# MLP blocks of a hybrid decoder step: which of VectorE and GpSimd makes the activations' sums, and which the weights'

## The chip, the cores and the metric

The kernel runs on one core of a Trainium2 chip. The metric is the device time of one execution in microseconds, and a version's time is the median over its runs. Engines are named as the profile names them: PE is TensorE (matmuls; PEld its weight loads), DVE is VectorE, ACT is ScalarE, POOL is GpSimd, SP is SyncE, which only issues DMAs here.

## What is computed

One layer of a decoder on 1024 prompt rows and 64 sample rows of width 1024, in float32: attention and a pooling branch, merged and projected, then an MLP. Only the MLP matters here. In the reference it is one line:

```
f = jnp.square(jax.nn.relu(rms_norm(h, g_pre_mlp) @ w_mlp_up)) @ w_mlp_down
return h + rms_norm(f, g_post_mlp)
```

The hidden width is 4096.

## The kernel before

Every float32 operand of a matmul is split into a high part (a copy rounded to the engine's fp32r type) and a low part (value minus high part), and each product is made of three matmuls: high by high, high by low, low by high. ACT makes high parts (tiles `wfh`, `wdh`), DVE low parts (`wfl`, `wdl`).

The MLP's hidden width is taken in blocks of 256 columns: 14 of them (`N_WINO`, the first written out, the other 13 in a loop on each engine), and a remainder of 4 tiles of 128 after them in the plain way. In a block, PE first makes the hidden activations (`wino_up`, six products of 8 input tiles), ACT applies relu and square (`wino_hidden`) into `wff`, and then PE multiplies them by two 128-row tiles of the down weights (`wino_downs`). This second product is made by Strassen's scheme in Winograd's form. For each of four groups `i` of row tiles it takes the four activation tiles A11, A12, A21, A22 and the four weight tiles B11 to B22, forms four sums of each (S1 to S4 from A, T1 to T4 from B), and needs seven products instead of eight. A product is named `(number, i)`: (5, 0) is product 5 of group 0. The sums are made in this kernel as follows.

- Of the activations: `wino_sums(w, i, squares)` on POOL, four additions of 128x128 elements for each group, 16 in a block. Group 3 needs the last squares of the block (`squares` 6), groups 1 and 2 those of the fourth product (4), group 0 those of the second (2).
- Of the weights: `wino_weight_sums(w)` on DVE, four additions of 128x512 elements in a block, once the weights have landed in `wdf`.

The results of the seven products leave PSUM in two ways. DVE adds five kinds of result into `acc` (`wino_add`). ACT copies the others into four small buffers `tmp` (`wino_copy`), from which POOL adds them into `acc` (`wino_pool_add`).

Each group has two PSUM banks, and products follow one another in them. So PE waits inside `wino_downs` before some products until a result was taken out: product (3, 0) waits for DVE's addition of (5, 0), product (6, 0) for ACT's copy of (1, 0). PE makes its products in pairs in this order: (1,0)(5,0), (1,1)(5,1), (6,0)(3,0), (6,1)(3,1), and so on; a pair is six matmuls of 512 columns.

Every engine executes its instructions in the order in which they are written, and waits on semaphores. `w_sq` counts ACT's squares, `w_sum` the activation sums, `wd_in` the weights' DMA, `wd_sum` the weight sums, `w_add` DVE's additions, `w_copy` ACT's copies. There is no scheduler: the order is that of the text.

Of the kernel before, what the change touches and what calls it, by code (L numbers as in the profile page):

```python
# [64 lines left out]
N_UP = len(W_UPS)  # L65
# [10 lines left out]
W_A21, W_A11, W_A22, W_A12, W_S1, W_S2, W_S3, W_S4 = range(8)  # L76
W_B12, W_B11, W_B21, W_B22, W_T1, W_T2, W_T3, W_T4 = range(8)
# [72 lines left out]
def build(nc, I, O):  # L150
    f32, f32r = mybir.dt.float32, mybir.dt.float32r
    ALU, ACT = mybir.AluOpType, mybir.ActivationFunctionType
    ctx = ExitStack()
    with ctx:
# [3 lines left out]
        def at(name, shape, off, dt=f32):  # L158
            return nc.alloc_sbuf_tensor_at(name, shape, dt, offset=16512 + off)
# [79 lines left out]
        wdf = at("wdf", [P, 8, 512], R32 + 16384)  # L239
        wfl = at("wfl", [P, 4, 8, P], R24, f32r)  # L240
        wff = at("wff", [P, 4, 8, P], R24)
# [27 lines left out]
        def sem(name):  # L269
            return ctx.enter_context(nc.semaphore(name))  # L270
# [28 lines left out]
        w_up, w_relu, w_sq, w_sum, w_fh, w_fl = (sem("w_" + n) for n in ("up", "relu", "sq", "sum", "f_hi", "f_lo"))  # L299
        wd_in, wd_sum, wd_hi, wd_lo = (sem("wd_" + n) for n in ("in", "sum", "hi", "lo"))  # L300
# [176 lines left out]
        def _(pool):  # L477
# [4 lines left out]
                               base=0, pattern=[[-1, P]], channel_multiplier=1).then_inc(ident_set, 1)  # L482
# [5 lines left out]
                               base=P - 1, pattern=[[-1, P]], channel_multiplier=-1).then_inc(consts, 1)  # L488
# [48 lines left out]
            def window(src, scratch, w, width, at_col):  # L537

                span, cur, n, i = 1, src, width + w - 1, 0
                base = at_col - (w - 1)  # L540
                while span < w:
                    n -= span
                    chained(pool.tensor_tensor(scratch[i % 2](0, n), cur(base + span, n), cur(base, n), ALU.add))
                    cur, base, span, i = scratch[i % 2], 0, 2 * span, i + 1
                return cur
# [8 lines left out]
            for t in range(PT_):  # L554
                w = 2 ** (t + 1)
                for c, (c0, width) in enumerate(CH):
                    width = min(width, SEQ - c0)
                    pool.wait_ge(freed["A"], FREED[g_in(U_UP + t, c)][1])
                    s = window(lambda a, n: upp[:, t, a:a + n], row, w, width, PSTATE + c0)
# [10 lines left out]
                s = window(lambda a, n: ups[:, t, :, a:a + n], per_seq, w, T_DEC, PSTATE)  # L570
# [29 lines left out]
            for i in range(3):  # L600
                pool.wait_ge(h_out[i], 16 * 3)

            def wino_sums(w, i, squares):

                a = lambda s: wff[:, i, s, :]
                base = w * 16 + 4 * i
                pool.wait_ge(w_sq, w * N_UP + squares)
                pool.tensor_tensor(a(W_S1), a(W_A21), a(W_A22), ALU.add).then_inc(w_sum, 1)  # L608
                pool.tensor_tensor(a(W_S3), a(W_A11), a(W_A21), ALU.subtract).then_inc(w_sum, 1)
                pool.wait_ge(w_sum, base + 1)  # L610
                pool.tensor_tensor(a(W_S2), a(W_S1), a(W_A11), ALU.subtract).then_inc(w_sum, 1)
                pool.wait_ge(w_sum, base + 3)
                pool.tensor_tensor(a(W_S4), a(W_A12), a(W_S2), ALU.subtract).then_inc(w_sum, 1)

            def wino_pool_add(w, m, first):

                number, i = m
                r = W_ROWS[i][0] if number == 4 else W_ROWS[i][1]
                k = W_COPIED[m]
                if number == 2:  # L620
                    pool.wait_ge(w_pool, w * N_COPY + (W_COPIED[(1, i)] + 1))
                pool.wait_ge(w_copy, copied_of(w, m))
                a = acc[:, r, 0:512]
                if first and number != 2:
                    pool.tensor_copy(a, tmp[k % N_TMP][:, :]).then_inc(w_pool, 1)
                else:
                    pool.tensor_tensor(a, a, tmp[k % N_TMP][:, :], ALU.add).then_inc(w_pool, 1)  # L627

            def wino_pool(w, first=False):
                wino_sums(w, 0, 2)  # L630
                wino_sums(w, 1, 4)
                wino_sums(w, 2, 4)
                wino_sums(w, 3, 6)
                wino_pool_add(w, (1, 0), first)
                wino_pool_add(w, (1, 1), first)
                wino_pool_add(w, (2, 0), first)
                wino_pool_add(w, (2, 1), first)
                wino_pool_add(w, (1, 2), first)
                wino_pool_add(w, (4, 0), first)
                wino_pool_add(w, (4, 1), first)  # L640
                wino_pool_add(w, (1, 3), first)
                wino_pool_add(w, (2, 2), first)
                wino_pool_add(w, (2, 3), first)
                wino_pool_add(w, (4, 2), first)
                wino_pool_add(w, (4, 3), first)
# [389 lines left out]
        def _(dve):  # L1035
# [299 lines left out]
            def wino_low(w, i):  # L1335
                dve.wait_ge(w_fh, w * 5 + (W_LO[i] + 1))
                if i == "sample":
                    dve.tensor_tensor(wsb[:, :, 1, :], wsf[:, :, :], wsb[:, :, 0, :].bitcast(f32), ALU.subtract)\
                        .then_inc(w_fl, 1)
                else:  # L1340
                    dve.tensor_tensor(wfl[:, i, 1:8, :], wff[:, i, 1:8, :], wfh[:, i, :, :].bitcast(f32), ALU.subtract)\  # L1341
                        .then_inc(w_fl, 1)

            def wino_weight_sums(w):
                b = lambda s: wdf[:, s, :]
                dve.wait_ge(wd_in, w * 32 + 32)
                dve.tensor_tensor(b(W_T1), b(W_B12), b(W_B11), ALU.subtract).then_inc(wd_sum, 1)
                dve.tensor_tensor(b(W_T3), b(W_B22), b(W_B12), ALU.subtract).then_inc(wd_sum, 1)
                dve.wait_ge(wd_sum, w * 4 + 1)
                dve.tensor_tensor(b(W_T2), b(W_B22), b(W_T1), ALU.subtract).then_inc(wd_sum, 1)  # L1350
                dve.wait_ge(wd_sum, w * 4 + 3)
                dve.tensor_tensor(b(W_T4), b(W_B21), b(W_T2), ALU.subtract).then_inc(wd_sum, 1)

            def wino_weights_low(w, half):
                s = slice(4 * half, 4 * half + 4)
# [5 lines left out]
            def wino_lo(w, s):  # L1361
                dve.wait_ge(w_hi, w * 2 + (U_W + 2 + s + 1))
                dve.tensor_tensor(wr[:, (s + 1) % 2, 1, :], raw[:, s, :], wr[:, (s + 1) % 2, 0, :].bitcast(f32),
                                  ALU.subtract).then_inc(w_lo, 1)

            def wino_add(w, m, first):

                number, i = m
                r = W_ROWS[i][1] if number in (6, 3) else W_ROWS[i][0]
                if number in (3, 7):  # L1370
                    dve.wait_ge(w_add, added_of(w, (6 if number == 3 else 5, i)))
                dve.wait_ge(w_done, done_of(w, m))
                a = acc[:, r, 512:]
                if first and number in (5, 6):
                    dve.tensor_copy(a, ps[:, wino_bank(m), :]).then_inc(w_add, 1)
                else:
                    dve.tensor_tensor(a, a, ps[:, wino_bank(m), :], ALU.add).then_inc(w_add, 1)  # L1377
# [7 lines left out]
                    dve.tensor_tensor(a, a, ps[:, 4:6, :], ALU.add).then_inc(w_add, 1)  # L1385

            def wino_from_lows(w, first=False):
                wino_low(w, 1)
                wino_low(w, 2)
                wino_low(w, "sample")  # L1390
                if first:
                    for i in range(3):
                        dve.wait_ge(h_out[i], 16 * 3)
                wino_add(w, (5, 0), first)
                wino_add(w, (5, 1), first)
                wino_add(w, (6, 0), first)
                wino_add(w, (3, 0), first)
                wino_add(w, (6, 1), first)
                wino_add(w, (3, 1), first)
                wino_add(w, (7, 0), first)  # L1400
                wino_add(w, (7, 1), first)
                wino_low(w, 3)
                wino_add(w, (5, 2), first)
                wino_lo(w, 0)
                wino_add(w, (5, 3), first)
                wino_add(w, (6, 2), first)
                wino_add(w, (3, 2), first)
                wino_add(w, (6, 3), first)
                wino_add(w, (3, 3), first)
                wino_add(w, (7, 2), first)  # L1410
                wino_add(w, (7, 3), first)
                wino_lo(w, 1)
                wino_sample_add(w, first)
# [4 lines left out]
            n_low(7)  # L1418
            normed(8)
            dve.wait_ge(done, G_M)  # L1420
            wino_weight_sums(0)
            n_low(8)
            wino_weights_low(0, 0)
            wino_low(0, 0)
# [1 line left out]
            dve.sem_inc(w_add, 1)  # L1426
            wino_from_lows(0, True)
            with dve.Fori(1, N_WINO) as w:
                wino_weight_sums(w)
                wino_weights_low(w, 0)  # L1430
                wino_low(w, 0)
                wino_weights_low(w, 1)
                wino_from_lows(w)
# [45 lines left out]
            for half, (ready, freeing) in enumerate(((y_half, y_part), (done, freed["D"]))):  # L1479
                cols = slice(half * 512, half * 512 + 512)  # L1480
                dve.wait_ge(ready, 1 if half == 0 else down_done(n))
                a, before_it = acc[:, r, cols], D0 + n
# [592 lines left out]
```

## Time and profile before

| | us |
|---|---|
| median of 3 runs | 1324.61 (1323.03 to 1325.12) |
| the profiled execution, its own time | 1320.92 |
| its span in the trace (first to last instruction) | 1319.2 |
| busy: PE | 1304.9 (99% of the span) |
| busy: DVE, ACT, POOL | 697.5, 569.2, 450.4 |

The span covers the instructions, and the execution's own time has 1.7 us around it. Busy time is the sum of an engine's instructions; that of PE is a model of overlapping matmuls, so 99% says that matmuls followed one another closely. PE's granted clock was 0.996 of full speed over the span.

### The profile page before, as it was taken

The page shows a single profiled execution, that of the slowest core. Times are in us where ns is not written, and L with a number is a line of the kernel's source. Part 1 is how long each engine was busy: PE and PEld are TensorE (multiplying, and loading weights), DVE is VectorE, ACT ScalarE, POOL GpSimd, SP SyncE. Part 2 cuts the span into 40 slices and gives each one's busy share as a digit, 9 for nine tenths or more (in the row PEclk, how much of TensorE's full clock was granted, in tenths as well). Part 3 has the DMA queues.
Part 4 walks back from the last instruction along what each step waited for, and adds up shares of the span by engine and source line. Part 5 has one row for each costly group of instructions (what it writes and reads, how often), then busy time and mean ns, then how long its engine had stood idle before and what let it go on. Part 6 is the DMA issues. An engine that isn't in the chain of part 4 may idle for free.

```text
span 1319.2 us, 20373 instructions
## 1 busy us (share of the span) xinstructions
PE 1304.9 (99%) x7483; PEld 1204.9 (91%) x7483; DVE 697.5 (53%) x1071; ACT 569.2 (43%) x1063; POOL 450.4 (34%) x541
## 2 busy tenths in 40 slices
PE   8999999999999999999999999999999999999998
PEld 7999889999999998889988998999899989998986
DVE  7488833222222245547567556656665666566256
ACT  7365524111111144436445544554455445544532
POOL 4002771000000001104466456645654575457010
PEclk9999989999999999999999999999999999999999
DMA  8200001111111125330110111011101110110152
GB/s 269 87 33 33 33 18 37 49 48 46 35 49 48 49 75 188 108 130 12 64 64 0 64 64 64 0 64 64 62 1 64 64 44 20 64 64 32 65 194 93
DMA packets 23638, 84.42 MB, mean 64 GB/s; under 512 B 3202, under 2 KB 3282, under 8 KB 23562
## 3 DMA queue, kind: packets, MB, share of 16 engines
q1 hardware_dynamic: 17968, 64.30, 13.9%
q0 software_dynamic: 5472, 19.12, 4.6%
q8 instruction: 37, 0.61, 0.2%
q10 hardware_dynamic: 146, 0.27, 0.1%
q14 instruction: 15, 0.12, 0.0%
HBM read 74.38 MB, written 10.39 MB: 64 GB/s over the span
## 4 chain that ended last, share of the span: by engine, by line
PE 94%; DVE 3%; ACT 2%; issue 1%; DMA 0%; DVEq 0%; ACTq 0%
PE ps L1878 20%; PE ps L1511 19%; PE ps L1512 19%; PE ps L1513 19%; PE ps L1753 9%; PE ps L1911 2%; PE ps L1532 2%; DVE pr L1153 1%; PE ps L1761 1%; ACT pr L771 1%; PE ps L1727 1%; PE ps L1670 0%; DVE pr L1191 0%; DMA xrow<-in_x_prompt 0%; PE ps L1828 0%
## 5 line engine op out<-in xcount | busy, mean ns | idle before, releaser
L1511 PE MATMUL ps<-xn,wr 128*128 128x384 f32 (+1 forms) x1360 | 448.1, 329 | 0.0
L1512 PE MATMUL ps<-xn,wr 128*128 128x384 f32 (+1 forms) x1360 | 445.9, 328 | 0.0
L1513 PE MATMUL ps<-xn,wr 128*128 128x384 f32 (+1 forms) x1360 | 445.6, 328 | 0.0
L1511 PEld LDWEIGHTS ps<-xn,wr 128*128 128x128 f32 x1360 | 256.8, 189 | 1.0
L1512 PEld LDWEIGHTS ps<-xn,wr 128*128 128x128 f32 x1360 | 256.8, 189 | 0.6
L1513 PEld LDWEIGHTS ps<-xn,wr 128*128 128x128 f32 x1360 | 256.6, 189 | 0.0
L627 POOL TENSOR_TENSOR acc<-acc,tmp 128x512 f32<-128x512 f32 x160 | 239.5, 1518 | 46.6 <-ACT tmp L947 44.7
L1377 DVE TENSOR_TENSOR acc<-acc,ps 128x512 f32<-128x512 f32 x216 | 143.4, 685 | 37.8 <-PE ps L1878 31.2
L947 ACT ACTIVATE tmp<-ps 128x512 f32<-128x512 f32 x168 | 97.2, 597 | 150.8 <-PE ps L1878 120.3
L1878 PE MATMUL ps<-wdh,wfh 128*128 128x512 f32 x392 | 130.4, 390 | 0.0
L1878 PE MATMUL ps<-wdl,wfh 128*128 128x512 f32 x392 | 130.1, 390 | 0.0
L1878 PE MATMUL ps<-wdh,wfl 128*128 128x512 f32 x392 | 129.8, 389 | 0.0
L1039 DVE TENSOR_TENSOR wr<-raw,wr 128x1024 fp32r<-128x1024 f32 x36 | 44.5, 1236 | 143.3 <-ACT wr L666 143.3
L608 POOL TENSOR_TENSOR wff<-wff 128x128 f32<-128x128 f32 x56 | 35.2, 628 | 214.7 <-ACT wff L919 175.0
L911 ACT ACTIVATE fa<-ps 128x384 f32<-128x384 f32 (+1 forms) x84 | 39.8, 474 | 147.0 <-PE ps L1513 147.0
L582 POOL DMA_DIRECT2D g<-in_vectors x3 | 1.7, 566 | 280.6 <-DVE mix L1224 267.2
L1341 DVE TENSOR_TENSOR wfl<-wff,wfh 128x896 fp32r<-128x896 f32 x56 | 65.0, 1173 | 59.8 <-ACT wfh L928 59.8
L1359 DVE TENSOR_TENSOR wdl<-wdf,wdh 128x2048 fp32r<-128x2048 f32 x28 | 64.2, 2292 | 56.1 <-ACT wdh L936 56.1
L1878 PEld LDWEIGHTS ps<-wdh,wfl 128*128 128x128 f32 x392 | 73.6, 188 | 15.7
L1878 PEld LDWEIGHTS ps<-wdl,wfh 128*128 128x128 f32 x392 | 73.6, 188 | 15.4
L1878 PEld LDWEIGHTS ps<-wdh,wfh 128*128 128x128 f32 x392 | 73.0, 188 | 14.8 <-ACT tmp L947 0.4
L1753 PE MATMUL ps<-wo,xn 128*128 128x512 f32 x336 | 77.7, 390 | 0.0
(280 smaller groups left out, 1835.9 us busy)
## 6 DMA issues: line engine op xcount, KB each, us to landing
raw<-in_weights SPq DMA_DIRECT2D x78, 512.0 KB, 4.1
wdf<-in_weights SPq DMA_DIRECT2D x28, 512.0 KB, 4.1
xrow<-in_x_prompt SPq DMA_DIRECT2D x8, 512.0 KB, 8.6
xr<-in_x_prompt POOLq DMA_DIRECT2D x8, 512.0 KB, 5.4
residual_rows<-h POOLq DMA_DIRECT2D x8, 512.0 KB, 2.9
hb<-residual_rows POOLq DMA_DIRECT2D x8, 512.0 KB, 9.8
out_y_prompt<-hb SPq DMA_DIRECT2D x7, 512.0 KB, 2.6
g<-in_vectors POOLq DMA_DIRECT2D x3, 512.0 KB, 4.0
```

The source lines that it names most:

```text
L627: pool.tensor_tensor(a, a, tmp[k % N_TMP][:, :], ALU.add).then_inc(w_pool, 1)
L911: act.activation(f[:, 0:width], ps[:, W_BANK[i], 0:width], ACT.Relu).then_inc(w_relu, 1)
L947: act.activation(tmp[k % N_TMP][:, :], ps[:, wino_bank(m), :], ACT.Copy).then_inc(w_copy, 1)
L1039: dve.tensor_tensor(lo_, raw[:, n % 2, :], hi_.bitcast(f32), ALU.subtract).then_inc(w_lo, 1)
L1341: dve.tensor_tensor(wfl[:, i, 1:8, :], wff[:, i, 1:8, :], wfh[:, i, :, :].bitcast(f32), ALU.subtract)\
L1359: dve.tensor_tensor(wdl[:, s, :], wdf[:, s, :], wdh[:, s, :].bitcast(f32), ALU.subtract).then_inc(wd_lo, 1)
L1377: dve.tensor_tensor(a, a, ps[:, wino_bank(m), :], ALU.add).then_inc(w_add, 1)
L1511: pe.matmul(out, wh, rh, start=(i == 0), stop=False)
L1512: pe.matmul(out, wh, rl, start=False, stop=False)
L1513: mm = pe.matmul(out, wl, rh, start=False, stop=(i == last))
L1753: mm = [pe.matmul(out[:, half, :], s, m[:, half * 512:(half + 1) * 512], start=start, stop=stop) for half in range(2)]
L1878: return pe.matmul(ps[:, wino_bank(m), :], s, v, start=number in (1, 5, 2) and part == 0, stop=part == 2, skip_group_check=True)
```

## The change

The two helpers change places. POOL's text gets `wino_weight_sums` at the head of each block, and loses the four calls of `wino_sums`. DVE's text loses `wino_weight_sums`, and gets `wino_sums` in four places: group 0 where the weight sums were, groups 1 and 2 ahead of their low parts, and group 3 behind the low part of the samples, ahead of the block's first addition. The sums themselves are the same. ACT's and PE's texts are unchanged.

```
 POOL:
+            def wino_weight_sums(w):
+                b = lambda s: wdf[:, s, :]
+                pool.wait_ge(wd_in, w * 32 + 32)
+                pool.tensor_tensor(b(W_T1), b(W_B12), b(W_B11), ALU.subtract).then_inc(wd_sum, 1)
+                pool.tensor_tensor(b(W_T3), b(W_B22), b(W_B12), ALU.subtract).then_inc(wd_sum, 1)
+                pool.wait_ge(wd_sum, w * 4 + 1)
+                pool.tensor_tensor(b(W_T2), b(W_B22), b(W_T1), ALU.subtract).then_inc(wd_sum, 1)
+                pool.wait_ge(wd_sum, w * 4 + 3)
+                pool.tensor_tensor(b(W_T4), b(W_B21), b(W_T2), ALU.subtract).then_inc(wd_sum, 1)
...
             def wino_pool(w, first=False):
-                wino_sums(w, 0, 2)
-                wino_sums(w, 1, 4)
-                wino_sums(w, 2, 4)
-                wino_sums(w, 3, 6)
+                wino_weight_sums(w)
                 wino_pool_add(w, (1, 0), first)
                 wino_pool_add(w, (1, 1), first)
...
 DVE:
+            def wino_sums(w, i, squares):
+
+                a = lambda s: wff[:, i, s, :]
+                base = w * 16 + 4 * i
+                dve.wait_ge(w_sq, w * N_UP + squares)
+                dve.tensor_tensor(a(W_S1), a(W_A21), a(W_A22), ALU.add).then_inc(w_sum, 1)
+                dve.tensor_tensor(a(W_S3), a(W_A11), a(W_A21), ALU.subtract).then_inc(w_sum, 1)
+                dve.wait_ge(w_sum, base + 1)
+                dve.tensor_tensor(a(W_S2), a(W_S1), a(W_A11), ALU.subtract).then_inc(w_sum, 1)
+                dve.wait_ge(w_sum, base + 3)
+                dve.tensor_tensor(a(W_S4), a(W_A12), a(W_S2), ALU.subtract).then_inc(w_sum, 1)
...
             def wino_from_lows(w, first=False):
+                wino_sums(w, 1, 4)
+                wino_sums(w, 2, 4)
                 wino_low(w, 1)
                 wino_low(w, 2)
                 wino_low(w, "sample")
+                wino_sums(w, 3, 6)
...
             with dve.Fori(1, N_WINO) as w:
-                wino_weight_sums(w)
+                wino_sums(w, 0, 2)
                 wino_weights_low(w, 0)
```

How DVE's instructions stand in the loop, from the samples' low part (`wsb`) to the additions of (5, 0) and (5, 1) into `acc`. Before:

```order
L1338 TENSOR_TENSOR wsb<-wsf,wsb 128x2x64 [waits w_f_hi]
L1372 ISA
L1377 TENSOR_TENSOR acc<-acc,ps 128x512 [waits w_product]
L1372 REGISTER_ALU
L1377 TENSOR_TENSOR acc<-acc,ps 128x512 [waits w_product]
```

With the change, at the same place:

```order
L1333 TENSOR_TENSOR wsb<-wsf,wsb 128x2x64 [waits w_f_hi]
L1343 REGISTER_ALU
L1344 TENSOR_TENSOR wff<-wff 128x128 [waits w_sq]
L1345 TENSOR_TENSOR wff<-wff 128x128
L1346 REGISTER_ALU
L1347 TENSOR_TENSOR wff<-wff 128x128 [waits w_sum]
L1348 REGISTER_ALU
L1349 TENSOR_TENSOR wff<-wff 128x128 [waits w_sum]
L1369 ISA
L1374 TENSOR_TENSOR acc<-acc,ps 128x512 [waits w_product]
```

Group 3's four sums (S1, S3, S2, S4 in this order) now stand between the samples' low part and the addition of (5, 0).

How POOL's instructions stand in the loop, at the end of group 3's sums and the first two additions from `tmp`, which are those of (1, 0) and (1, 1). Before:

```order
L607 REGISTER_ALU
L608 TENSOR_TENSOR wff<-wff 128x128 [waits w_sq]
L609 TENSOR_TENSOR wff<-wff 128x128
L610 REGISTER_ALU
L611 TENSOR_TENSOR wff<-wff 128x128 [waits w_sum]
L612 REGISTER_ALU
L613 TENSOR_TENSOR wff<-wff 128x128 [waits w_sum]
L622 ISA
L627 TENSOR_TENSOR acc<-acc,tmp_125 128x512 [waits w_copied]
L622 REGISTER_ALU
L627 TENSOR_TENSOR acc<-acc,tmp_126 128x512 [waits w_copied]
```

With the change, the whole head of POOL's loop:

```order
L606 TENSOR_TENSOR wdf<-wdf 128x512 [waits wd_in]
L607 TENSOR_TENSOR wdf<-wdf 128x512
L608 ISA
L609 TENSOR_TENSOR wdf<-wdf 128x512 [waits wd_sum]
L610 REGISTER_ALU
L611 TENSOR_TENSOR wdf<-wdf 128x512 [waits wd_sum]
L620 ISA
L625 TENSOR_TENSOR acc<-acc,tmp_125 128x512 [waits w_copied]
L620 REGISTER_ALU
L625 TENSOR_TENSOR acc<-acc,tmp_126 128x512 [waits w_copied]
```

Nothing stands between the weight sums and the additions from `tmp` any more, so the addition of (1, 0) waits for ACT's copy alone.

## Rows read from the trace of the kernel before

**Rows 1.** The page, busy time and the chain that ended last

```profile
PE 1304.9 (99%) x7483; PEld 1204.9 (91%) x7483; DVE 697.5 (53%) x1071; ACT 569.2 (43%) x1063; POOL 450.4 (34%) x541
...
PE 94%; DVE 3%; ACT 2%; issue 1%; DMA 0%; DVEq 0%; ACTq 0%
```

**Rows 2.** What PE waited for, longest first: us in total, times, longest

```profile
PE ps L1532 <- DVE pr L1191: 2.5, 4, 1.3
```

**Rows 3.** Single lines: durations in ns (min/median/max), first and last start in us

```profile
L608 POOL TENSOR_TENSOR wff<-wff x56: 460/462/1859, 601.2 to 1196.7; 128x128 f32<-128x128 f32 x56
...
L627 POOL TENSOR_TENSOR acc<-acc,tmp x160: 1286/1298/2289, 623.6 to 1218.3; 128x512 f32<-128x512 f32 x160
...
L1377 DVE TENSOR_TENSOR acc<-acc,ps x216: 674/687/690, 620.6 to 1212.9; 128x512 f32<-128x512 f32 x108
...
L1138 DVE TENSOR_TENSOR vd<-vr x7: 283/284/291, 59.6 to 60.9; 128x128 f32<-128x128 f32 x7
...
L1338 DVE TENSOR_TENSOR wsb<-wsf,wsb x14: 309/313/314, 617.7 to 1197.0; 128x128 fp32r<-128x128 f32 x14
```

**Rows 4.** Timeline of DVE in one block: start us, us, what [idle before]

```profile
840.34 0.31 DVE L1338 TENSOR_TENSOR wsb<-wsf,wsb 128x128 fp32r<-128x128 f32 x1 [0.89 <-ACT wsb L925]
840.57 0.68 DVE L1377 TENSOR_TENSOR acc<-acc,ps 128x512 f32<-128x512 f32 x1
```

**Rows 5.** Timeline of PE in the same block, the pair (6, 0) and (3, 0)

```profile
841.26 0.39 PE L1878 MATMUL ps<-wdh,wfl 128*128 128x512 f32 x1
841.49 0.61 PE L1878 MATMUL ps<-wdh,wfh 128*128 128x512 f32 x2
```

**Rows 6.** Timeline in the first block: PEld's waits, and DVE's copy of (5, 0)

```profile
617.90 0.68 DVE L1375 COPY acc<-ps 128x512 f32<-128x512 f32 x1
...
618.63 0.19 PEld L1878 LDWEIGHTS ps<-wdh,wfh 128*128 128x128 f32 x1 [0.27 <-DVE acc L1375]
618.74 0.19 PEld L1878 LDWEIGHTS ps<-wdl,wfh 128*128 128x128 f32 x1
```

**Rows 7.** Timeline of ACT: copies of (1, 0), (1, 1) and (2, 0)

```profile
840.21 0.58 ACT L947 ACTIVATE tmp<-ps 128x512 f32<-128x512 f32 x1
841.46 0.60 ACT L947 ACTIVATE tmp<-ps 128x512 f32<-128x512 f32 x1 [0.68 <-PE ps L1878]
...
845.77 0.60 ACT L947 ACTIVATE tmp<-ps 128x512 f32<-128x512 f32 x1 [1.89 <-PE ps L1878]
```

**Rows 8.** Timeline of POOL: the addition of (2, 0)

```profile
846.45 1.30 POOL L627 TENSOR_TENSOR acc<-acc,tmp 128x512 f32<-128x512 f32 x1 [1.99 <-ACT tmp L947]
```

**Rows 9.** Timeline in the first block: DVE and POOL additions side by side

```profile
600.79 0.68 DVE L1347 TENSOR_TENSOR wdf<-wdf 128x512 f32<-128x512 f32 x1
601.39 0.95 DVE L1348 TENSOR_TENSOR wdf<-wdf 128x512 f32<-128x512 f32 x1
...
601.15 0.64 POOL L608 TENSOR_TENSOR wff<-wff 128x128 f32<-128x128 f32 x1 [2.52 <-DMA residual_rows<-h]
601.76 0.90 POOL L609 TENSOR_TENSOR wff<-wff 128x128 f32<-128x128 f32 x1
```

**Rows 10.** Timeline of the block of rows 4, its earlier part: DVE and POOL

```profile
820.55 0.69 DVE L1347 TENSOR_TENSOR wdf<-wdf 128x512 f32<-128x512 f32 x1 [5.45 <-DMA wdf<-in_weights]
...
824.78 0.46 POOL L608 TENSOR_TENSOR wff<-wff 128x128 f32<-128x128 f32 x1 [6.47 <-ACT wff L919]
...
826.63 2.29 DVE L1359 TENSOR_TENSOR wdl<-wdf,wdh 128x2048 fp32r<-128x2048 f32 x1 [3.46 <-ACT wdh L936]
829.74 1.09 DVE L1341 TENSOR_TENSOR wfl<-wff,wfh 128x896 fp32r<-128x896 f32 x1 [0.82 <-ACT wfh L928]
...
837.31 2.13 DVE L1341 TENSOR_TENSOR wfl<-wff,wfh 128x896 fp32r<-128x896 f32 x2 [3.47 <-ACT wfh L928]
```

**Rows 11.** Stretches: us, busy of PE, PEld, DVE, ACT, POOL; then PE's granted clock

```profile
180.00:185.60 5.60, 5.60 (x68) 4.86 (x66) 0.30 (x1) 0.58 (x1) 5.12 (x7) 1.00 0.30 97
185.60:192.50 6.90, 6.90 (x37) 6.67 (x38) 0.42 (x1) 0.38 (x1) 4.88 (x6) 0.51 0.00 0
```

More of the change, by code:

```diff
@@ L601, in _ @@
                 pool.wait_ge(h_out[i], 16 * 3)
[L603 to L613, printed above, removed]
+            def wino_weight_sums(w):
[7 more added lines that the diff above has]
+                pool.tensor_tensor(b(W_T4), b(W_B21), b(W_T2), ALU.subtract).then_inc(wd_sum, 1)
             def wino_pool_add(w, m, first):
@@ L1342, in wino_low @@
                         .then_inc(w_fl, 1)
[L1344 to L1352, printed above, removed]
+            def wino_sums(w, i, squares):
[8 more added lines that the diff above has]
+                dve.tensor_tensor(a(W_S4), a(W_A12), a(W_S2), ALU.subtract).then_inc(w_sum, 1)
             def wino_weights_low(w, half):
@@ L1420, in _ @@
             dve.wait_ge(done, G_M)
-            wino_weight_sums(0)
+            wino_sums(0, 0, 2)
             n_low(8)
```

## The prediction

> **What bounds the kernel now.** I read the page's busy times first. PE is busy for 99% of the span and makes 94% of the chain that ended last [rows 1]. Next comes the list of PE's waits: its largest entry is 2.5 us, and it lies in the attention part, not in the MLP [rows 2]. So PE's own work sets the time. Work taken off DVE, ACT or POOL gains nothing, and the only question is whether the change makes PE wait. The 13 blocks of the loop repeat very evenly: the samples' low part, once per block, takes 309 to 314 ns each time and runs from 617.7 to 1197.0, which is 44.6 us per block [rows 3]. So one block, read closely, speaks for 13.
>
> Where could PE wait? The place to look at is its third pair, (6, 0)(3, 0). The first matmul of (6, 0) starts at 841.49; two in a row take 0.61 and one alone 0.39, so that of (3, 0) starts at 841.49 + 0.61 - 0.39 = 841.71 [rows 5]. The weights of (3, 0) are loaded beside the matmul in front, from 841.49 on, and this load carries the wait for DVE's addition of (5, 0). That addition runs from 840.57 to 841.25 [rows 4]. The first block shows what happens when it is late: the copy ends at 618.58, the weights start loading 0.05 later, marked as a wait on it, and the matmul starts with the next load, 0.11 later [rows 6]. So today's slack is 841.49 - 841.25 - 0.05 = 0.19 us, and behind it each microsecond on DVE is one on PE.
>
> **The change, part by part.**
>
> *Weight sums, DVE to POOL.* They start when the DMA has landed, at 820.55 [rows 10]. POOL has been idle since 824.78 - 6.47 = 818.31 [rows 10]. A 128x512 addition takes POOL 1.30 us against DVE's 0.69 [rows 3, 10]; four take about 4 x 1.25 + 0.2 = 5.2 us (successive ones overlap by some 0.05, and two wait for a result; an estimate), so they end near 825.8. The first reader is DVE's first low part of the weights at 826.63, and behind that DVE has another 0.82 us idle [rows 10]. Cost 0. What hides it is 0.8 + 0.8 us of other engines' work; were it gone, each microsecond would be one per block.
> The Trainium skill, GPSIMD Engine Reference, section Engine selection, advises against this half of the change: elementwise work on VectorE, since GpSimd is about twice as slow with two inputs. The rows agree on the ratio (1.30 to 0.69), and off the path it costs nothing.
>
> *Activation sums, POOL to DVE.* A 128x128 addition takes DVE 0.28 us [rows 3]. The next one starts 0.08 us before the end of the one in front, as the addition at 840.57 does before 840.65 [rows 4], so a step is 0.20, and 0.31 where it waits for the result in front. Four take about 0.9 us. Group 0 goes where the weight sums were: its squares are ready at 824.7, since POOL takes them up at 824.78 [rows 10]. POOL's fourth weight sum may hold it up until 825.8, then it ends near 826.7, against 826.63; hidden by the 0.82 idle. Groups 1 and 2 fall into the 3.47 us that DVE idles ahead of 837.31 [rows 10] and need 1.8. Cost 0. Group 3 has no such gap: it stands between the samples' low part and the addition of (5, 0).
>
> *Group 3 with nothing in the way.* S1 takes the place of the addition, 840.57; S3 840.77; S2 840.97; S4 waits for S2's end at 841.25 and runs 841.28 to 841.56; the addition starts at 841.48 and ends at 842.16. PE's matmul follows 0.05 + 0.11 later, at 842.32 instead of 841.71: 0.6 us per block.
>
> *Group 3 beside POOL.* But POOL is no longer busy with these sums. Its first addition from `tmp`, today behind them, waits only for ACT's copy, which ends at 840.79 [rows 7]. POOL starts 0.08 after a copy, as 846.45 follows 845.77 + 0.60 [rows 7, 8], so at 840.87, in the middle of the sums.
> What two such operations do to one another is seen in the first block, where both engines have two inputs in SBUF [rows 9]. DVE's addition from 600.79 ends at 601.47. POOL's from 601.15 takes 0.64 instead of 0.46 [rows 3] and ends at 601.79, 0.32 after DVE's. DVE's next starts at 601.39, takes 0.95 instead of 0.69 and ends at 602.34, 0.55 after POOL's. POOL's next ends at 602.66, again 0.32 after that. So each holds the other out to its end, in turn, even where DVE had its next instruction queued already; and an operation needs whatever is shared only 0.14 us after its start (0.46 - 0.32, and 0.69 - 0.55). DVE's additions out of PSUM are not touched: 216 of them take 674 to 690 ns [rows 3].
> The Trainium skill, SBUF — State Buffer, section SBUF: two separate sides, says the same of a DVE operation with two SBUF inputs and a GpSimd one: an exclusive lock for the whole instruction, to the one that starts first. By it the sum is the one that follows, about 1360; without it, 1332.
> Carried through: S1 ends at 840.85, S3 holds until 841.06. POOL's (1, 0) asks at 841.01, S2 at 841.11, so POOL goes first and holds 1.30 - 0.14 = 1.16, to 842.22. S2 ends at 842.36. ACT's copy of (1, 1) ends at 842.06 [rows 7]; POOL starts (1, 1) at 842.17, just before the end of (1, 0), and asks at 842.31. S4 asks only at 842.53, for it waits for S2. So POOL takes the second turn, to 843.52, S4 ends at 843.66, the addition of (5, 0) runs 843.58 to 844.26, and PE's matmul comes at 844.42 instead of 841.71. Cost 2.7 us per block. The bounds are 0.6 (no contention) and 2.7 (two turns; POOL has no third addition ready before PE goes on). I take the upper one, since the rows of the first block are the same kind of pair.
>
> *Behind it.* Waits after this point hang on PE's own later products and move with it. DVE has (5, 1) done by 844.9, and PE's pair (6, 1)(3, 1) then stands near 845.5. The next block starts with every engine in the same relation to PE. Nothing takes up the 2.7 us, for PE is idle nowhere in the block.
>
> *First block.* PE waits there already [rows 6], and its first additions are copies. Between 0 and 2.7; I take 0.5.
>
> *Sum.* 13 x 2.7 + 0.5 = 35.6 us. On the profiled execution (1320.9) that is 1356.5; on the median, 3.7 us above it, 1324.6 + 35.6 = 1360.
>
> **The rivals.**
>
> *One turn only (B).* If POOL's (1, 1) asks after S4, that is 0.22 us later than worked out, the addition ends one hold earlier. S4 then ends at 842.67, the addition at 843.27, the matmul comes at 843.43: 1.7 us per block, 13 x 1.7 + 0.5 = 22.6, 1347. For it: the margin is small. Against: the copies' times repeat within nanoseconds from block to block, as the low part's durations suggest.
>
> *No contention (C).* If the short sums slip through, 13 x 0.6 = 7.8, 1332. For it: 0.28 us operations are much shorter than any that the rows show held up on DVE. Against: POOL's 0.46 us ones were held up.
>
> *Not slower (D).* The addition of (5, 0) has 0.19 us of slack. If DVE finished the four sums that much earlier, or they cost under 0.19 in all, PE would not wait, and the first block's wait, which hangs partly on POOL's late sums, would go: 1324.1. It decides at 0.05 us per sum, against a step of 0.20. Hardly possible.
>
> *The clock falls (E).* PE would idle 2.7 us at once in each block, more than the four waits of the largest entry of its list together [rows 2]. At 185.6 to 192.5 the granted clock was 0.51, the lower level of 1.2 GHz [rows 11]; such a fall costs half of 6.9, 3.4 us. Against: ahead of this fall, from 180 to 185.6, PE was not waiting but busy with 68 small matmuls at a clock of 1.00, 2.4 GHz [rows 11], so the trace ties no fall to a single wait, nor does it rule one out. If it fell in a third of the blocks: 4.3 x 3.4 = 15 more, 1375; in all of them 45 more, 1405.
>
> **How the numbers follow.** Chances: two turns 0.50, B 0.14, C 0.12, D 0.05, E 0.19. The likeliest gives 1360. The range 1343 to 1385 holds the first two and most of E (0.14 of 0.19), 0.78 in all; C and D lie below it, the worst of E above. The likeliest case alone has 1355 to 1366: 0.2 us of error per block is 2.6. A measurement of this kernel tells about 0.2%, 2.6 us, from no change. Only D is not beyond it: faster 0.01, same 0.04, slower 0.95.
>
> **What would show it.** In the list of PE's waits: a new entry, DVE's `acc` addition, 13 or 14 times, 2.5 to 2.7 us each, and block lengths of 47.3 instead of 44.6. On DVE: S2 and S4 of group 3 at about 1.4 us each instead of 0.28, S1 and S3 plain. On POOL: (1, 0) starting 0.53 us after the samples' low part. Weight sums on POOL at 1.3 us each, with nobody waiting for them. C would show four plain sums and PE waits of 0.6, B one long S2 or S4 and 1.7, E a granted clock under 1.00 in the MLP. I would be wrong if PE waited for `wdl` or `wfl` instead, or if DVE kept the shared side through its chain of sums.

## The result, and the profile after

The changed kernel takes 1365.69 us (median of 4 runs, 1362.74 to 1367.65) against 1324.38 for the kernel before: a ratio of 1.0319, interval 1.0305 to 1.0333, 41.3 us more. Forecast were 1360 and slower. Ratios are estimated together with their intervals, and can differ in the last digit from the quotient of two medians. Four executions ran in a slow state (1449.86 and 1890.97 us in two of the experiments, 2625.2 and 3365.72 of the kernel before beside them) and are left out of all times and ratios.

The page, busy time and the chain that ended last, as in [rows 1]:

```profile
PE 1315.1 (96%) x7483; PEld 1208.6 (89%) x7483; DVE 747.7 (55%) x1239; ACT 568.9 (42%) x1063; POOL 412.7 (30%) x373
...
PE 89%; DVE 5%; ACT 3%; issue 2%; DMA 1%; DVEq 0%; SPq 0%; ACTq 0%
```

PE has the same 7483 matmuls, but its share fell from 99% to 96%, and DVE now has 5% of the chain. The list of PE's waits, as in [rows 2], names the place:

```profile
PE ps L1878 <- DVE acc L1374: 30.7, 13, 2.4
...
PE ps L1878 <- DVE acc L1372: 0.6, 1, 0.6
```

There are 13 waits for DVE's addition into `acc`, one for each block of the loop, and a short one in the first block. The list counts from the modelled end of the matmul in front, so its 2.4 us is less than a block loses by the wait (2.7 us, below). Here is the place in one block, on DVE, as in [rows 4]:

```profile
856.56 0.29 DVE L1333 TENSOR_TENSOR wsb<-wsf,wsb 128x128 fp32r<-128x128 f32 x1 [0.93 <-ACT wsb L920]
856.77 0.28 DVE L1344 TENSOR_TENSOR wff<-wff 128x128 f32<-128x128 f32 x1
856.97 0.28 DVE L1345 TENSOR_TENSOR wff<-wff 128x128 f32<-128x128 f32 x1
857.17 1.37 DVE L1347 TENSOR_TENSOR wff<-wff 128x128 f32<-128x128 f32 x1
858.58 1.23 DVE L1349 TENSOR_TENSOR wff<-wff 128x128 f32<-128x128 f32 x1
859.74 1.27 DVE L1374 TENSOR_TENSOR acc<-acc,ps 128x512 f32<-128x512 f32 x2
```

And on POOL, as in [rows 8]:

```profile
857.09 1.30 POOL L625 TENSOR_TENSOR acc<-acc,tmp 128x512 f32<-128x512 f32 x1 [15.10 <-ACT tmp L942]
...
858.36 1.30 POOL L625 TENSOR_TENSOR acc<-acc,tmp 128x512 f32<-128x512 f32 x1
```

Read them side by side. S1 and S3 take their plain 0.28 us. POOL's addition of (1, 0) starts at 857.09, while S3 is in work, and ends at 858.39; S2, started at 857.17, ends at 858.54. POOL's addition of (1, 1) ends at 859.66, S4 at 859.81. Each of the two sums ends 0.15 us after an addition of POOL. The addition of (5, 0) starts 3.18 us after the samples' low part, instead of 0.23 [rows 4]. PE feels it like this, as in [rows 5], one block earlier:

```profile
810.43 0.39 PE L1878 MATMUL ps<-wdh,wfh 128*128 128x512 f32 x1
813.18 0.50 PE L1878 MATMUL ps<-wdh,wfh 128*128 128x512 f32 x1 [2.36 <-DVE acc L1374]
```

The matmul of (3, 0) starts 2.75 us after that of (6, 0), where it was 0.22, and takes 0.50 us itself instead of 0.39. The samples' low parts of these two blocks stand 856.56 - 809.27 = 47.29 us apart, against 44.6 before:

```profile
809.27 0.29 DVE L1333 TENSOR_TENSOR wsb<-wsf,wsb 128x128 fp32r<-128x128 f32 x1 [0.93 <-ACT wsb L920]
...
905.33 0.29 DVE L1333 TENSOR_TENSOR wsb<-wsf,wsb 128x128 fp32r<-128x128 f32 x1 [0.93 <-ACT wsb L920]
```

The last row is the block after them: it stands 905.33 - 856.56 = 48.77 us behind, 1.5 us more than 47.29.

That block is one of four with another mark: PE's granted clock. The columns are those of [rows 11].

```profile
716.92:720.34 3.42, 3.18 (x8) 2.51 (x9) 1.73 (x4) 1.52 (x2) 0.00 (x0) 0.50 0.00 0
860.28:863.70 3.42, 3.23 (x8) 2.56 (x9) 1.73 (x4) 1.47 (x2) 0.00 (x0) 0.50 0.00 0
1003.64:1007.06 3.42, 3.33 (x8) 2.66 (x9) 1.73 (x4) 1.36 (x2) 0.00 (x0) 0.50 0.00 0
1147.00:1150.42 3.42, 3.36 (x8) 2.69 (x9) 1.73 (x4) 1.34 (x2) 0.00 (x0) 0.50 0.00 0
```

In every third block PE ran at the lower level (0.50, 1.2 GHz) for 3.42 us. Each stretch begins 0.06 to 0.24 us before PE's wait ends (3.42 less PE's busy time in it), and PE starts 8 matmuls in it. At full clock matmuls start 0.227 us apart, so 14 or 15 would fit. The four blocks with a fall are 48.73 to 48.83 us long and the others, behind the first, 47.25 to 47.29 (from the starts of the samples' low parts), so a fall costs 1.5 us, 6.0 in all.

The first block costs little. PE's second product starts there at 615.25 and in the next block at 660.38, 45.13 us later. With the change it starts at 618.80 and 664.38, 45.58 us apart: 0.45 more.

So the 41.3 us are 13 x 2.7 = 35 of waiting, 6.0 of clock and about 0.5 in the first block; the sum is 41.5. What lies ahead of the MLP differs by a few us between executions, whatever the kernel: that second product starts at 615.81 in the first experiment below and at 618.88 in the last, whose texts agree up to there, and the runs of the kernel before go from 1317.94 to 1326.04. It is left aside.

### The profile page after: what moved, and what is told of

Read it like the earlier page. It is cut to its first block, busy times and chain, and to the rows that moved or that the text cites. A ratio compares the mean times of both kernels' runs of the same rounds, so it can differ in the third digit from the quotient of the medians.

```text
span 1364.1 us, 20373 instructions
## 1 busy us (share of the span) xinstructions
PE 1315.1 (96%) x7483; PEld 1208.6 (89%) x7483; DVE 747.7 (55%) x1239; ACT 568.9 (42%) x1063; POOL 412.7 (30%) x373
## 4 chain that ended last, share of the span: by engine, by line
PE 89%; DVE 5%; ACT 3%; issue 2%; DMA 1%; DVEq 0%; SPq 0%; ACTq 0%
PE ps L1511 18%; PE ps L1512 18%; PE ps L1513 18%; PE ps L1878 17%; PE ps L1753 9%; PE ps L1532 2%; PE ps L1911 2%; DVE wff L1347 1%; DVE pr L1148 1%; PE ps L1761 1%; DMA xrow<-in_x_prompt 1%; DVE acc L1374 1%; ACT pr L766 1%; PE ps L1727 1%; ACT fa L906 0%
## 5 line engine op out<-in xcount | busy, mean ns | idle before, releaser
L1878 PE MATMUL ps<-wdh,wfh 128*128 128x512 f32 x392 | 136.9, 402 | 31.4 <-DVE acc L1374 30.7
L1374 DVE TENSOR_TENSOR acc<-acc,ps 128x512 f32<-128x512 f32 x216 | 142.5, 684 | 41.3 <-PE ps L1878 34.7
L1344 DVE TENSOR_TENSOR wff<-wff 128x128 f32<-128x128 f32 x56 | 25.7, 458 | 125.3 <-ACT wff L914 125.3
L1753 PEld LDWEIGHTS ps<-wo,xn 128*128 128x128 f32 x336 | 63.0, 188 | 13.4
```

The costliest lines, as they stand in the source:

```text
L1753: mm = [pe.matmul(out[:, half, :], s, m[:, half * 512:(half + 1) * 512], start=start, stop=stop) for half in range(2)]
L1878: return pe.matmul(ps[:, wino_bank(m), :], s, v, start=number in (1, 5, 2) and part == 0, stop=part == 2, skip_group_check=True)
```

## The experiments

**Group 3's sums alone given back to GpSimd.** In the changed kernel:

```
 POOL, wino_pool:
                 wino_weight_sums(w)
+                wino_sums(w, 3, 6)
                 wino_pool_add(w, (1, 0), first)
 DVE, wino_from_lows:
                 wino_low(w, "sample")
-                wino_sums(w, 3, 6)
```

> The changed kernel with the sums of group 3 alone given back to GpSimd, where they stand behind the weight sums and ahead of the first addition from tmp; the sums of groups 0 to 2 stay on VectorE and the weight sums on GpSimd. Theory (the loss comes from group 3's sums alone, which VectorE makes in turns with GpSimd's additions): nothing is left of it, 1324 us, no entry in PE's list of waits for VectorE's additions in the loop, granted clock 1.00 in the MLP. Rival (weight sums on GpSimd, or the other sums on VectorE, carry a part): between 1330 and 1365, with PE waiting for wdl or wfl. Rival (any move of work off GpSimd's queue lets its additions collide with VectorE): some of the 2.7 us per block stays.

1322.05 us, ratio to the kernel before 0.9998 (0.998 to 1.0015). Nothing of the loss is left, and the clock stays at full speed. The other 12 sums on DVE and the weight sums on POOL, together, cost nothing.

**Group 3's sums alone on VectorE.** In the kernel before:

```
 POOL, wino_pool:
                 wino_sums(w, 2, 4)
-                wino_sums(w, 3, 6)
 DVE, wino_from_lows:
                 wino_low(w, "sample")
+                wino_sums(w, 3, 6)
```

> The kernel before, with group 3's sums alone moved to VectorE, to the place that the change gives them; everything else, the weight sums on VectorE too, as before. Theory: the whole loss, as in the changed kernel: 13 x 2.7 = 35, and some 1.5 us for each block in which the granted clock falls, so 1360 to 1367. Rival (the loss needs the weight sums on GpSimd as well, or the other groups on VectorE): clearly less, 1332 if only the 0.6 us of the longer queue counts.

1367.27 us, ratio 1.032 (1.0295 to 1.0344), the whole loss. The waits of PE in the loop are the same to the last digit:

```profile
PE ps L1890 <- DVE acc L1388: 30.7, 13, 2.4
```

The clock fell here too, for 3.42 us in each of four blocks, every third (from 719.17, 862.53, 1005.89 and 1149.25). The first block waits 1.6 us instead of 0.6.

**The weight sums alone on GpSimd.** In the kernel before:

```
 POOL, wino_pool:
+                wino_weight_sums(w)
                 wino_sums(w, 0, 2)
 DVE, loop and first block:
-                wino_weight_sums(w)
```

> The kernel before, with the weight sums alone moved to GpSimd, ahead of its activation sums; VectorE loses them and gets nothing. Theory: four additions of 1.3 us that end before anyone needs them, and GpSimd's additions from tmp still behind its own sums: 1324, same as before. Rival (GpSimd's slower additions are felt): group 0's sums start about 1 us later and ScalarE's high part with them; if that reached PE, up to 1 us per block, 1337.

1334.06 us, ratio 1.0083 (1.006 to 1.0107). The theory gave 1324 and was wrong. POOL's list had room for the weight sums, but the activation sums behind them now start later and meet DVE's low parts, which have two inputs in SBUF as well. In the first block POOL comes to its second activation sum just when DVE starts a long low part; the first two rows are DVE's and POOL's, and the third, from PE's weight loads, shows what came of it:

```profile
607.70 2.47 DVE L1360 TENSOR_TENSOR wdl<-wdf,wdh 128x2048 fp32r<-128x2048 f32 x1 [0.58 <-POOL wdf L611]
...
607.98 2.51 POOL L619 TENSOR_TENSOR wff<-wff 128x128 f32<-128x128 f32 x1
...
620.48 0.50 PEld L1877 LDWEIGHTS ps<-wdh,wfh 128*128 128x128 f32 x2 [4.04 <-issue]
```

A sum of 0.46 us took 2.51, and it ended 0.32 after DVE's low part. PE's weight loads stood still for 4 us at the start of the second product. The profile names no releaser for that wait ("issue"); that the first block's weight sums bring it is shown by the next run, which has them on VectorE and no such wait. PE's clock was 0.50 for 6.8 us, from 0.8 us before the wait ended:

```profile
619.70:626.50 6.80, 5.99 (x14) 4.77 (x15) 3.29 (x5) 3.66 (x8) 3.64 (x7) 0.50 0.00 0
```

In the loop, too, sums meet low parts. Group 0's last sum falls behind one of the weights and takes 2.39 us (first row, POOL). Everything behind it on POOL comes later, and the last sum of group 2 meets the low part of group 1 (rows of DVE, POOL and ACT):

```profile
836.56 2.39 POOL L623 TENSOR_TENSOR wff<-wff 128x128 f32<-128x128 f32 x1
...
847.00 1.09 DVE L1352 TENSOR_TENSOR wfl<-wff,wfh 128x896 fp32r<-128x896 f32 x1 [2.93 <-ACT wfh L939]
...
847.11 1.30 POOL L623 TENSOR_TENSOR wff<-wff 128x128 f32<-128x128 f32 x1
...
848.44 0.95 ACT L939 ACTIVATE wfh<-wff 128x896 fp32r<-128x896 f32 x1 [1.48 <-POOL wff L623]
```

ACT idles 1.48 us for it, and what ACT does next is late too: PE's weight loads now wait in each block of the loop for ACT's copy (up to 0.4 us) and for DVE's addition (up to 0.3). The blocks are about 0.4 us longer (45.0).

**The same, in the loop only,** with the first block's weight sums left on VectorE:

```
 POOL, wino_pool:
+                if not first:
+                    wino_weight_sums(w)
                 wino_sums(w, 0, 2)
```

> The run with the weight sums alone on GpSimd took 10 us more than before. Here they are on GpSimd in the 13 blocks of the loop, and on VectorE in the first block as before. Theory (two losses: in the first block GpSimd starts late and its sums meet VectorE's low parts, one long wait of PE and a fall of the granted clock, 4 to 6 us; in each block of the loop group 2's last sum meets VectorE's low part of group 1, 0.37 us): 13 x 0.37 = 5, 1329, no fall of the clock near the first block. Rival (all of it comes from the first block and its echo in the later ones): 1324. Rival (all from the loop): 1334.

1327.46 us, ratio 1.0047 (1.0024 to 1.007). The samples' low part again gives the blocks: (1203.8 - 617.4) / 13 = 45.1.

```profile
L1350 DVE TENSOR_TENSOR wsb<-wsf,wsb x14: 307/311/313, 617.4 to 1203.8; 128x128 fp32r<-128x128 f32 x14
```

By the two ratios, the 11 us of the run before fall into 6 of the loop (uncertain by 3) and 5 of the first block (by 4). No long wait and no fall of the clock is left in the first block, and the ratio is above 1 by more than its interval, so both losses exist. The loss in the loop was expected a little lower (0.37 a block, now 0.5).

**GpSimd's additions held until group 3's sums are done.** In the changed kernel, one wait more:

```
 POOL, wino_pool:
                 wino_weight_sums(w)
+                pool.wait_ge(w_sum, w * 16 + 16)
                 wino_pool_add(w, (1, 0), first)
```

> The changed kernel with one wait more on GpSimd: its first addition from tmp waits until group 3's four sums are done (w_sum), so that none of its additions can run beside them. Nothing is taken away; GpSimd starts later. Theory (turns at something shared): the sums take 0.28 us each again and only the longer queue counts, 0.6 us per block, 13 x 0.6 = 8, 1332, granted clock 1.00. Rival (the sums are slow on VectorE by themselves, or the place in the queue is the cost): 1365 as in the changed kernel, since VectorE's and PE's texts are the same.

1333.31 us, ratio 1.0071 (1.0053 to 1.0089). One wait more takes 32 us off. VectorE:

```profile
802.52 0.29 DVE L1345 TENSOR_TENSOR wff<-wff 128x128 f32<-128x128 f32 x1
802.73 0.28 DVE L1346 TENSOR_TENSOR wff<-wff 128x128 f32<-128x128 f32 x1
802.93 0.28 DVE L1348 TENSOR_TENSOR wff<-wff 128x128 f32<-128x128 f32 x1
803.25 0.29 DVE L1350 TENSOR_TENSOR wff<-wff 128x128 f32<-128x128 f32 x1
803.46 1.28 DVE L1375 TENSOR_TENSOR acc<-acc,ps 128x512 f32<-128x512 f32 x2
```

All four sums are plain: from the first one's start to that of the addition it is 0.94 us, against 0.9 worked out from a step of 0.20. What is left, 0.6 us per block, is the price of the place in the queue.

**Only the second addition held.** The same wait ahead of `wino_pool_add(w, (1, 1), first)` instead:

> The changed kernel with GpSimd's second addition from tmp, (1, 1), held until group 3's sums are done; its first, (1, 0), runs as it likes. Theory (the two engines take turns, and each of GpSimd's additions that falls among the sums costs one hold of 1.16 us, less what the plain chain takes): one turn instead of two, S2 long and S4 plain, 1.6 to 1.7 us of waiting per block, 13 x 1.65 = 21, 1346, plus at most a few us if the granted clock still falls. Rival (one turn costs all, the second is hidden): 1360 to 1365. Rival (only the second counts): 1332.

1347.11 us, ratio 1.0169 (1.0144 to 1.0194). One sum is long, the other plain:

```profile
853.27 1.37 DVE L1348 TENSOR_TENSOR wff<-wff 128x128 f32<-128x128 f32 x1
854.67 0.29 DVE L1350 TENSOR_TENSOR wff<-wff 128x128 f32<-128x128 f32 x1
```

So each addition of POOL among the sums is one turn. Two turns, one and none give 41, 22 and 9 us. In the profiled execution of this run the granted clock never fell in the MLP, so its 22 us are waiting alone; of the 41 us, 6.0 are clock.

**Matmuls that fill PE's wait.** In the changed kernel, in the pair (6, 0)(3, 0); the ten products are written to a bank that is overwritten later and are used for nothing, and the wait on `w_relu`, which counts ACT's relus, keeps them off what ACT has still to read:

```
                 wino_term(m, 0)
...
+                if fill:
+                    pe.wait_ge(w_relu, w * N_UP + 3)
+                    for _ in range(fill):
+                        pe.matmul(ps[:, 0, :], wfh[:, 0, 0, :], wdh[:, 1, :], start=True, stop=True, skip_group_check=True)
                 bank_read(w, n)
```

> The changed kernel with ten matmuls of 512 columns more in each block on PE, between the first product of (6, 0) and the wait for VectorE's addition of (5, 0); they go to a PSUM bank whose content is overwritten later, so they only fill 10 x 0.227 = 2.3 of the 2.7 us for which PE waits there. Theory (the 2.7 us are a wait of PE, and the part of the loss beyond them is the granted clock falling behind it): the block keeps its 47.3 us, the clock stays at 1.00, and the time is some 6 us below the changed kernel's 1365.7: 1360, in spite of 140 matmuls more. Rival (the falls have nothing to do with PE standing still): 1365 and four falls again. Rival (PE is not really idle there): 32 us more, 1397.

1357.94 us, ratio 1.0249 (1.0224 to 1.0275): 140 matmuls more and 7.8 us less than the changed kernel, from three executions that go from 1355.3 to 1362.2. PE, and PEld's wait that is left:

```profile
858.52 2.43 PE L1898 MATMUL ps<-wdh,wfh 128*128 128x512 f32 x10
861.08 0.50 PE L1878 MATMUL ps<-wdh,wfh 128*128 128x512 f32 x1
...
861.08 0.19 PEld L1878 LDWEIGHTS ps<-wdh,wfh 128*128 128x128 f32 x1 [0.56 <-DVE acc L1374]
```

The blocks and the clock in the MLP (first and last of the samples' low parts; then a stretch with the columns of [rows 11], first of this run, then of the changed kernel):

```profile
L1333 DVE TENSOR_TENSOR wsb<-wsf,wsb x14: 292/293/293, 620.9 to 1235.5; 128x128 fp32r<-128x128 f32 x14
...
600.00:1300.00 700.00, 698.24 (x3679) 636.44 (x3679) 445.10 (x613) 338.38 (x584) 318.44 (x226) 1.00 0.13 45
```

```profile
L1333 DVE TENSOR_TENSOR wsb<-wsf,wsb x14: 292/293/293, 620.4 to 1239.2; 128x128 fp32r<-128x128 f32 x14
...
600.00:1300.00 700.00, 668.64 (x3515) 610.29 (x3514) 442.24 (x610) 335.44 (x579) 317.99 (x226) 0.99 0.13 45
```

With the fill, the 13 block lengths between these low parts are 614.6 us together, against 618.8, and the clock is 1.00. The 4.2 us less are the 6.0 of the falls less some 1.4 in the first block (46.98 us to the next low part instead of 45.63), where ten matmuls take longer than the short wait that they fill. The rest of the 7.8 us is no more than executions differ by. The mean granted clock of the whole span speaks for the other executions: 0.989 to 0.994 in the changed kernel and with group 3's sums alone on VectorE, 0.995 to 0.999 with the fill and in every other experiment (one of them has the single fall of 6.8 us told above). The busy share of PE is now full, and the kernel is hardly faster: busy time alone does not tell waiting from useless work.

**Group 3's sums behind the addition of (5, 0), GpSimd not held.** In the changed kernel:

```
 DVE, wino_from_lows:
                 wino_low(w, "sample")
-                wino_sums(w, 3, 6)
...
                 wino_add(w, (5, 0), first)
+                wino_sums(w, 3, 6)
                 wino_add(w, (5, 1), first)
```

> As the run with group 3's sums behind VectorE's addition of (5, 0), but without the hold on GpSimd: its additions from tmp start when ScalarE's copies are there. Theory (turns): GpSimd's (1, 0) holds the port from 841.01 on, S1 comes after it at 842.3, GpSimd's (1, 1) takes the next turn to 843.46, S3, S2 and S4 follow until 844.11, and VectorE's addition of (5, 1) ends at 844.7 where PE wants it at 842.85; PE now waits for (5, 1), 1.8 us per block, 13 x 1.8 = 23, 1348. Rival (the place behind (5, 0) is what makes the order free, the hold does nothing): 1324.

1346.86 us, ratio 1.0173 (1.0154 to 1.0192). Now S1 and S3 are the long ones, and the addition of (5, 1) is late:

```profile
852.17 0.68 DVE L1374 TENSOR_TENSOR acc<-acc,ps 128x512 f32<-128x512 f32 x1
852.77 1.17 DVE L1344 TENSOR_TENSOR wff<-wff 128x128 f32<-128x128 f32 x1
853.86 1.37 DVE L1345 TENSOR_TENSOR wff<-wff 128x128 f32<-128x128 f32 x1
855.15 0.28 DVE L1347 TENSOR_TENSOR wff<-wff 128x128 f32<-128x128 f32 x1
```

POOL's two additions and PE's waits:

```profile
852.49 2.59 POOL L625 TENSOR_TENSOR acc<-acc,tmp 128x512 f32<-128x512 f32 x2 [15.46 <-ACT tmp L942]
...
PE ps L1878 <- DVE acc L1374: 20.1, 13, 1.5
```

DVE's addition of (5, 0), from 852.17 to 852.85, has one input in PSUM. It runs beside POOL's for the last 0.36 us and keeps its plain 0.68. S3 ends at 855.23, 0.15 us after POOL's second addition. So what is held out are the sums with both inputs in SBUF.

**The same, and GpSimd held.** Both edits together: the sums behind (5, 0), and the wait on `w_sum` ahead of POOL's first addition.

> The change in a better order: weight sums on GpSimd and activation sums on VectorE as in the changed kernel, but group 3's sums stand behind VectorE's addition of (5, 0) instead of ahead of it, and GpSimd's first addition from tmp waits for them. Theory: the addition of (5, 0) is as early as before, the sums take 0.9 us plain, the addition of (5, 1) ends near the moment at which PE needs it (0.4 us later than before, in a slack of about 0.4), and in the first block the wait of 0.5 us goes, since ScalarE no longer waits for GpSimd's sums: 1324, within 0.1 per block, so the whole change costs nothing. If the addition of (5, 1) is late by 0.1 to 0.2 us per block: 1326. Rival (VectorE's sums cost PE time wherever they stand): over 1330.

1321.64 us, ratio 0.9989 (0.9976 to 1.0003): not to be told from the kernel before. DVE:

```profile
843.70 0.68 DVE L1375 TENSOR_TENSOR acc<-acc,ps 128x512 f32<-128x512 f32 x1
844.30 0.28 DVE L1345 TENSOR_TENSOR wff<-wff 128x128 f32<-128x128 f32 x1
844.50 0.29 DVE L1346 TENSOR_TENSOR wff<-wff 128x128 f32<-128x128 f32 x1
844.70 0.28 DVE L1348 TENSOR_TENSOR wff<-wff 128x128 f32<-128x128 f32 x1
845.02 0.29 DVE L1350 TENSOR_TENSOR wff<-wff 128x128 f32<-128x128 f32 x1
845.23 1.43 DVE L1375 TENSOR_TENSOR acc<-acc,ps 128x512 f32<-128x512 f32 x2
```

The exchange of the two engines as such costs nothing, and any gain is below what the runs tell. The hold alone leaves 9 us, the new place alone 23.

## Why the prediction was right

*What bounds.* PE's own work, as forecast. The only new entries among its waits in the MLP are those for DVE's additions; the two versions without them (group 3 back on POOL, and sums behind (5, 0) with the hold) are back at the old time. The time of 1365.69 lies in the forecast range (1343 to 1385) and 5.7 us above the likeliest 1360.

*Weight sums on POOL at no cost.* Right in the changed kernel: nobody waits for them but S1 of group 0, as forecast, and with group 3 back on POOL nothing is left of the loss. But the cost of nothing rested on the activation sums having left POOL too. The two halves of the change are not independent: alone, the weight sums cost 11 us. The prediction priced only who waits for them, and not what stands behind them on POOL.

*Groups 0 to 2 at no cost.* Right. POOL's fourth weight sum did hold up S1 of group 0, as forecast, and the 0.8 us of idle time behind it remained:

```profile
840.96 1.17 DVE L1344 TENSOR_TENSOR wff<-wff 128x128 f32<-128x128 f32 x1 [9.64 <-ACT wff L914]
...
845.97 1.09 DVE L1336 TENSOR_TENSOR wfl<-wff,wfh 128x896 fp32r<-128x896 f32 x1 [0.81 <-ACT wfh L923]
```

*Group 3, 0.6 us for the place in the queue.* 0.6 measured: with POOL held, blocks of (1209.3 - 621.4) / 13 = 45.2 against 44.6.

```profile
L1334 DVE TENSOR_TENSOR wsb<-wsf,wsb x14: 293/293/293, 621.4 to 1209.3; 128x128 fp32r<-128x128 f32 x14
```

*Group 3, 2.7 us beside POOL.* 2.7 measured, by the mechanism forecast: turns, POOL first, S2 and S4 the ones held up, to 1.37 and 1.23 us. POOL's (1, 0) starts 0.53 us after the samples' low part, as worked out, and the addition of (5, 0) 3.18 us after it, where the working gives 3.24. The three runs with two, one and no turns carry it, and so does the run in which the sums' place was moved and other sums were hit. The Trainium skill, SBUF — State Buffer, section SBUF: two separate sides, states that of two such operations the one that starts first has the shared port pair for its whole instruction. The trace agrees: POOL's additions start at 857.09 and 858.36, S2 and S4 0.08 and 0.22 us later, and these end 0.15 us after them. No run here shows where in the chip the shared thing is, only which operations exclude one another.

*First block.* 0.5 forecast, 0.45 measured, partly by luck: the forecast was picked between 0 and 2.7 without a working. POOL's work there is a copy with one input (620.89 to 621.52), and it too held up a sum: S2, from 620.97, took 0.70 us.

*The clock.* This term was missing from the sum. It stood among the rivals (E) at 3.4 us in a third of the blocks, 15 in all. It fell in 4 of 13 blocks, as in that rival, but for 3.42 us at a time and not 6.9, at 1.5 us each: 6.0. The run with the fill shows that it is PE standing still: with the same waits filled with useless matmuls it did not fall. So the time lies between the likeliest case (1360) and E (1375), with the mechanism of both. That 1365.69 also lies within the 1355 to 1366 given to the likeliest case alone is luck, for the 6.0 us are no part of that case.

## What to carry to other kernels

Before work moves from one of VectorE and GpSimd to the other, list for each queue what its neighbours are at that moment: sums and low parts of VectorE with both inputs in SBUF, and GpSimd's work in SBUF (additions, and in the first block a copy), excluded one another here, from about 0.14 us after the start of the one (an estimate from [rows 9]) to its end. A chain of short sums beside long additions can so wait for a long one at each step. A queue that becomes free starts its next work earlier, and that can be the harm; a wait that orders the two engines can be worth more than the work moved (32 us here). Price the parts of an exchange alone too: here the weight sums alone cost 11 us and group 3's sums alone 43, while the weight sums together with the sums of groups 0 to 2 cost nothing.

## What the hardware showed that I had not expected

PE's granted clock fell to the lower level at waits of 2.4 us by PE's list (4 of 13, for 3.42 us each, in two profiled kernels alike), and in another at a wait of 3.8 us (for 6.8 us). Each fall began shortly before the wait ended. It never fell at 26 waits of 1.4 or 1.5 us in two other profiled executions, nor where matmuls filled the wait. Why it was every third block no run here shows.

The other thing is how fine the balance was before. In the kernel before, the last sum of group 2 starts 0.44 us ahead of the low part of group 1:

```profile
836.87 0.46 POOL L613 TENSOR_TENSOR wff<-wff 128x128 f32<-128x128 f32 x1
```

The low part starts at 837.31 [rows 10]. With the weight sums alone on POOL, the sum starts 0.11 us behind it (847.11 and 847.00). So a shift of 0.55 us between the two engines goes with blocks that are 0.4 us longer. No run varied that shift by itself.
